# Expert results kept on chip: each turn of three blocks is multiplied by a table of tokens and added to the residual, in place of stores to memory and a gather at the end

## The reference, cut to what matters

```python
group_logits = xt @ rg_w + rg_b                       # 4 groups of 8 experts
grp = argmax(group_logits)
top_val, top_idx = lax.top_k(expert_logits[grp], 2)   # 2 experts of that group for each token
gate = p_grp * jax.nn.softmax(top_val)
...
out = zeros; for each (token, expert) chosen:
    out[token] += gate * ((silu(x @ w_gate[e]) * (x @ w_up[e])) @ w_down[e])
x = x + out
return rmsnorm(x, final_norm_g)
```

## Time and profile before

| | |
|---|---|
| median of 3 runs | 2055.2 us (2052.13 to 2055.3) |
| the profiled execution's own time | 2054.98 us |
| its span, first to last instruction | 2053.7 us |
| PE (TensorE) busy | 1824.7 us, 89% |
| DVE (VectorE) busy | 863.6 us, 42% |
| POOL (GpSimd) busy | 992.7 us, 48% |
| ACT (ScalarE) busy | 432.7 us, 21% |
| DMA | 346.00 MB, mean 168 GB/s |

### The profile page before, as it was taken

One profiled execution on the slowest core, in us unless ns is written; L12 is line 12 of the kernel. 1 busy time (PEld: TensorE's weight loads), 2 busy tenths in 40 slices (PEclk: granted clock), 3 DMA queues, 4 the chain that ended last, 5 costly groups with the idle time before them and its releaser, 6 DMA issues.

```text
span 2053.7 us, 27415 instructions
## 1 busy us (share of the span) xinstructions
PE 1824.7 (89%) x9686; PEld 1287.1 (63%) x9686; DVE 863.6 (42%) x1256; ACT 432.7 (21%) x794; POOL 992.7 (48%) x536
## 2 busy tenths in 40 slices
PE   5999999989999899999999798996877978969783
PEld 4888888877776578888888666664642423323331
DVE  5444443410254567444444489877341111111113
ACT  3111100100244432111100143551321211111112
POOL 5888887767544278888888523321211111101101
PEclk9999999999999999999999999997868988988897
DMA  3333363423221123333333222210579999999983
GB/s 126 97 97 93 105 262 98 141 79 98 66 62 52 32 85 95 97 93 101 92 109 98 72 60 64 72 52 21 212 287 412 374 408 402 410 415 398 413 358 133
DMA packets 56977, 346.00 MB, mean 168 GB/s; under 512 B 8474, under 2 KB 8858, under 8 KB 44896
## 3 DMA queue, kind: packets, MB, share of 16 engines
q1 hardware_dynamic: 44640, 315.12, 42.1%
q10 hardware_dynamic: 7968, 19.46, 2.6%
q0 software_dynamic: 4320, 10.78, 1.5%
HBM read 475.06 MB, written 19.66 MB: 241 GB/s over the span
## 4 chain that ended last, share of the span: by engine, by line
PE 70%; DMA 13%; DVE 11%; ACT 3%; issue 1%; POOL 1%; SPq 0%; DVEq 0%; ACTq 0%; POOLq 0%
PE bank L460 31%; DMA big<-w_up_in 13%; PE bank L431 12%; PE bank L1760 7%; PE bank L692 4%; PE bank L1266 3%; DVE big L1043 3%; PE bank L1778 2%; PE bank L479 2%; PE bank L1376 2%; PE bank L1786 1%; PE bank L610 1%; DVE state L1028 1%; PE bank L670 1%; PE bank L1678 1%
## 5 line engine op out<-in xcount | busy, mean ns | idle before, releaser
L277 POOL TENSOR_TENSOR weights_hi_parts<-ring,ones 128x1024 fp32r<-128x1024 f32 (+1 forms) x176 | 356.6, 2026 | 304.7 <-PE bank L460 139.1
L279 POOL TENSOR_TENSOR ring_parts<-ring,weights_hi_parts 128x1024 fp32r<-128x1024 f32 (+1 forms) x176 | 473.9, 2693 | 13.8
L460 PE MATMUL bank<-attention_buffers_parts,weights_hi_parts 128*128 128x512 f32 x832 | 329.4, 396 | 27.9 <-POOL ring_parts L279 17.6
L460 PE MATMUL bank<-state_parts,weights_hi_parts 128*128 128x512 f32 x832 | 326.8, 393 | 0.0
L460 PE MATMUL bank<-attention_buffers_parts,ring_parts 128*128 128x512 f32 x832 | 326.7, 393 | 0.0
L1760 PE MATMUL bank<-big,work 128*32 128x512 f32 x1440 | 231.7, 685 | 54.5 <-DMA big<-w_up_in 54.4
L431 PE MATMUL bank<-big_parts,weights_hi_parts 128*128 128x512 f32 x704 | 217.1, 389 | 1.2 <-POOL ring_parts L279 1.2
L460 PEld LDWEIGHTS bank<-attention_buffers_parts,weights_hi_parts 128*128 128x128 f32 x832 | 158.1, 190 | 64.6 <-POOL ring_parts L279 17.6
L864 POOL TENSOR_TENSOR ring_parts<-ring,weights_hi_parts 128x1024 fp32r<-128x1024 f32 x32 | 81.0, 2534 | 234.1 <-ACT weights_hi_parts L861 234.1
L1860 POOL TENSOR_TENSOR small<-small 128x1 f32<-128x1 f32 x51 | 9.7, 190 | 381.3 <-DVE small L1683 381.3
L460 PEld LDWEIGHTS bank<-state_parts,weights_hi_parts 128*128 128x128 f32 x832 | 158.3, 190 | 33.4 <-issue 0.8
(11 more groups left out here) (377 smaller groups left out, 2827.1 us busy)
## 6 DMA issues: line engine op xcount, KB each, us to landing
big<-w_up_in SPq DMA_DIRECT2D x54, 2048.0 KB
ring<-wdense_in SPq DMA_DIRECT2D x176, 512.0 KB, 3.6
state<-w_down_in SPq DMA_DIRECT2D x37, 2048.0 KB
big<-w_gate_in SPq DMA_DIRECT2D x36, 2048.0 KB
attention_buffers<-w_gate_in SPq DMA_DIRECT2D x18, 2048.0 KB
ring<-w_down_in SPq DMA_DIRECT2D x18, 2048.0 KB
ring<-wff_in SPq DMA_DIRECT2D x32, 704.0 KB, 4.1
y_rows<-big ACTq DMA_DIRECT2D x1, 8192.0 KB, 28.0
```

The lines of the kernel that those rows point to most:

```text
L277: po.tensor_tensor(hi, raw, ones[:, 0:1].to_broadcast([128, words]), ALU.mult).then_inc(PO.sem, 1)
L279: po.tensor_tensor(lo, raw, hi.bitcast(F32), ALU.subtract) \
L460: m = pe.matmul(out, x, y_, start=j + n == 0, stop=j == len(pairs) - 1 and n == len(ts) - 1)
```

## The change

Nothing of the results goes to memory any more. `y_rows`, its filling, the 108 stores and the eight gathers are gone. In their place:

- **Tables.** After the routing, VectorE works out for each chosen (token, expert) pair its turn and its row of 96 in that turn. Two tables of hits are multiplied on TensorE once, which gives for each turn and row the token's number and its gate.
- **A one-hot for each turn** (`dve_hot`): 96 rows by 512 tokens, 1 where the row belongs to the token, in fp32r, by VectorE.
- **Results of a turn stay in SBUF** (`lap_y`, 96 rows by 1024). `add_odd` writes them with two VectorE instructions for a block (one before).
- **Split** (`split_lap`): GpSimd multiplies the turn's results by their gates, once into a high fp32r part and once in place, and subtracts, for each half of 512 features: six instructions a turn. They begin when the turn's third block has its sum, and `dve_result` of the next turn's first block waits for both halves (`s_split`), since it overwrites `lap_y`.
- **Products** (`lap_sums`): TensorE multiplies the one-hot by the high and the low part, for four groups of 128 tokens and two halves: 16 fp32r matmuls a turn into three PSUM banks in rotation. They are placed around the next turn's second and third block: n = 0, 1 before and n = 2, 3 behind `turn_products` of the second block, n = 4, 5 behind `gate_up` of the third, n = 6, 7 behind its `down`.
- **Adds** (`dve_add`): VectorE adds each of the eight products to the residual, eight instructions a turn. Products n = 2 and 3 wait for the adds of n = 0 and 1, whose banks they reuse.
- **Order of the loops.** The first turn's blocks stand ahead of the loops, the loops run once less, and the last turn's body is written out behind them. GpSimd's gathers go on between the splits.
- **The end.** The last turn's results are multiplied as plain fp32: VectorE puts the gates into the one-hot (`last_hot`), TensorE makes eight matmuls into eight banks, VectorE adds each with one instruction of 512 columns, and the final norm goes on as before.

```diff
+    lap_high = nc.alloc_sbuf_tensor_at("lap_results_high", [128, D], F32R, offset=lap_high_at)
...
-    zeros = big[:, 44 * T:44 * T + D]
-    cleared = PO.run(po.memset(zeros, 0.0))
...
-        if gain == "mix_norm":
-            AC.wait(cleared)
-            ac.dma_start(y_d.rearrange("(n p) c -> p n c", p=128),
-                         zeros.unsqueeze(1).to_broadcast([128, Y_ROWS // 128, D])).then_inc(s_fill, 16)
...
+    DV.run(dv.tensor_scalar(lap.bitcast(I32), place, 43691.0, None, ALU.mult))
+    DV.run(dv.tensor_scalar(lap.bitcast(I32), lap.bitcast(I32), 17, None, ALU.logical_shift_right))
+    DV.run(dv.tensor_copy(lap, lap.bitcast(I32)))
+    DV.run(dv.scalar_tensor_tensor(lap_row, lap, float(-SETS), place, ALU.mult, ALU.add))
+    DV.run(dv.scalar_tensor_tensor(lap_row, lap_row, float(BS), rmod, ALU.mult, ALU.add))
...
+        if c >= 2:
+            pe.wait_ge(s_added, i * 8 + {2: 7, 3: 8, 4: 11, 5: 15}[c])
...
-    def act_odd(i, c):
+    def act_odd(i, c, steps=1):
 
         ac.wait_ge(PE.sem, at_step(PE, PE_D, i, c + 1))
+        if c:
+            ac.wait_ge(DV.sem, at_step(DV, DV_Y, i, c))
         ac.activation(y_odd, results[c % SETS][2 * BS:4 * BS, :], ACT.Copy).then_inc(AC.sem, 1)
 
-    def act_store(i, c):
-
-        ac.wait_ge(DV.sem, at_step(DV, DV_Y, i, c + 1))
-        store(i, c)
-
-    def store(i, c):
+    def add_odd(c):
 
         for half in range(2):
-            ac.dma_start(y_d[bass.ds(i * (SETS * BS) + c * BS, BS), half * 512:half * 512 + 512],
-                         y_e[c % SETS][half * BS:(half + 1) * BS, :]).then_inc(s_y[c % SETS], 16)
+            p = slice(half * BS, (half + 1) * BS)
+            d = dv.tensor_tensor(lap_y[c % SETS * BS:(c % SETS + 1) * BS, half * 512:half * 512 + 512],
+                                 results[c % SETS][p, :], y_odd[p, :], ALU.add)
+        return d
 
     def dve_result(i, c, steps=1):
 
         dv.wait_ge(AC.sem, at_step(AC, AC_Y, i, c + 1))
-        dv.wait_ge(s_y[c % SETS], i * 32 + (32 * (c // SETS) + 16))
-        dv.tensor_tensor(y_e[c % SETS], results[c % SETS][0:2 * BS, :], y_odd, ALU.add).then_inc(DV.sem, steps)
+        if c == 3:
+            dv.wait_ge(s_split, i * 2 + 2)
+        add_odd(c).then_inc(DV.sem, steps)
+
+    def dve_hot(i, lap_at):
+
+        dv.tensor_copy(sel[0:LAP, :], tab[0:LAP, lap_at]).then_inc(s_sel, 1)
+        dv.wait_ge(s_sel, i)
+        dv.tensor_tensor(lap_hot_r.rearrange("p (t n) -> p t n", t=NT), iota_f[0:LAP, :].unsqueeze(1).to_broadcast([LAP, NT, 128]),
+                         sel[0:LAP, 0:NT].unsqueeze(2).to_broadcast([LAP, NT, 128]), ALU.is_equal).then_inc(s_hot, 1)
+
+    def split_lap(i):
+
+        po.wait_ge(DV.sem, at_step(DV, DV_Y, i, 3))
+        gate = sel[0:LAP, NT:NT + 1].to_broadcast([LAP, 512])
+        for half in range(2):
+            y, high, low = (x[0:LAP, half * 512:half * 512 + 512] for x in (lap_y, lap_high, lap_low))
+            po.tensor_tensor(high, y, gate, ALU.mult).then_inc(s_high, 1)
+            po.tensor_tensor(y, y, gate, ALU.mult).then_inc(s_high, 1)
+            po.wait_ge(s_high, i * 4 + (2 * half + 2))
+            po.tensor_tensor(low, y, high.bitcast(F32), ALU.subtract).then_inc(s_split, 1)
+
+    sum_banks = [results[b] for b in (1, 2, 1, 2, 2, 0, 2, 0)]
+
+    def lap_sums(i, first):
+
+        for n in (first, first + 1):
+            if n == 0:
+                pe.wait_ge(s_hot, i + 1)
+            if n % 4 == 0:
+                pe.wait_ge(s_split, i * 2 + (n // 4 + 1))
+            if n == 5:
+                pe.wait_ge(DV.sem, at_step(DV, DV_Y, i, 4))
+            if n in (2, 3, 4, 6, 7):
+                pe.wait_ge(s_added, i * 8 + {2: 9, 3: 10, 4: 12, 6: 13, 7: 14}[n])
+            t, half = n % 4, n // 4
+            for part in (lap_high, lap_low):
+                m = pe.matmul(sum_banks[n][:, :], lap_hot_r[:, t * 128:(t + 1) * 128],
+                              part[0:LAP, half * 512:half * 512 + 512], start=part is lap_high, stop=part is lap_low)
+            m.then_inc(s_prod, 1)
+
+    def dve_add(i, first):
+
+        for n in (first, first + 1):
+            dv.wait_ge(s_prod, i * 8 + (n + 1))
+            d = x_half(n % 4, n // 4)
+            dv.tensor_tensor(d, d, sum_banks[n][:, :], ALU.add).then_inc(s_added, 1)
...
+    for c in range(SETS):
+        rows_to_come(0, c)
     with po.Fori(0, laps["po"]) as i:
-        for c in range(SETS):
-            po.wait_ge(PO.sem, i * SETS + (gathers_begun + c))
-            po.wait_ge(DV.sem, at_step(DV, DV_IDX, i, c - 1))
-            po.tensor_tensor(zo, zc, zc, ALU.add).then_inc(PO.sem, 1)
-            gather(c, idx[c][0:BS, :])
+        rows_to_come(i, 3)
+        rows_to_come(i, 4)
+        split_lap(i)
+        rows_to_come(i, 5)
+    split_lap(laps["po"])
+    po.wait_ge(PO.sem, laps["po"] * SETS + (gathers_begun + SETS))
...
+    lap_hits, row_hits = ring[:, 0:C2 * LAPS], ring[:, 512:512 + C2 * LAP]
+    row_values = ring[:, 168:168 + 2 * C2 * LAPS]
+    assert C2 * LAPS <= 168 and 168 + 2 * C2 * LAPS <= 512 and 512 + C2 * LAP <= RING * SLOT - WE
     dve_rows(0, 0)
+    dv.tensor_tensor(by_slot(lap_hits), iota_f[:, 0:LAPS].unsqueeze(1).to_broadcast([128, C2, LAPS]),
+                     over_last(lap, C2, LAPS), ALU.is_equal).then_inc(s_hits, 1)
+    dv.tensor_tensor(by_slot(row_hits), iota_f[:, 0:LAP].unsqueeze(1).to_broadcast([128, C2, LAP]),
+                     over_last(lap_row, C2, LAP), ALU.is_equal)
+    dv.wait_ge(s_hits, 1)
+    for k, v in enumerate((tok_id, gates)):
+        d = dv.tensor_tensor(row_values.rearrange("p (c n k) -> p c n k", c=C2, k=2)[:, :, :, k], by_slot(lap_hits),
+                             over_last(v, C2, LAPS), ALU.mult)
+    d.then_inc(s_hits, 1)
     dve_mul(0, 0, 2)
+    dve_rows(0, 1)
+    dve_result(0, 0)
+    dve_mul(0, 1)
+    dv.wait_ge(s_tab, 1)
+    tab3, summed = tab[0:LAP, :].rearrange("p (n k) -> p n k", k=NT + 1), results[2][0:LAP, 0:2 * LAPS].rearrange("p (n k) -> p n k", k=2)
+    for t in range(NT):
+        dv.tensor_scalar(tab3[:, :, t], summed[:, :, 0], float(NO_ROW - 128 * t), None, ALU.add)
+    dv.tensor_copy(tab3[:, :, NT], summed[:, :, 1]).then_inc(s_hits, 1)
+    dve_rows(0, 2)
+    dve_result(0, 1)
+    dve_mul(0, 2)
+    dv.wait_ge(s_hits, 3)
+    dve_hot(1, slice(0, NT + 1))
...
+    def dve_lap(i, last=False):
+
+        dve_rows(i, 3)
+        dve_result(i, 2)
+        dve_mul(i, 3)
+        dve_rows(i, 4)
+        dve_result(i, 3)
+        dve_add(i, 0)
+        dve_mul(i, 4)
+        dve_add(i, 2)
+        dve_add(i, 4)
+        if not last:
+            dve_rows(i, 5)
+        dve_result(i, 4, 3 if last else 1)
+        dve_add(i, 6)
+        dve_mul(i, 5)
+        dve_hot(i + 2, bass.ds(i * (NT + 1) + (NT + 1), NT + 1))
     with dv.Fori(0, laps["dv"]) as i:
-        for c in range(1, SETS + 1):
-            dve_rows(i, c)
-            dve_result(i, c - 1)
-            dve_mul(i, c)
-    dve_rows(laps["dv"], 1)
-    dve_result(laps["dv"], 0)
-    dve_mul(laps["dv"], 1)
-    dve_result(laps["dv"], 1, 3)
-    dve_mul(laps["dv"], 2)
-    dv.wait_ge(AC.sem, at_step(AC, AC_SILU, laps["dv"], 2) + 1)
-    dv.wait_ge(s_y[2], laps["dv"] * 32 + 16)
-    dv.tensor_tensor(y_e[2], results[2][0:2 * BS, :], y_odd, ALU.add).then_inc(DV.sem, 1)
+        dve_lap(i)
+    dve_lap(laps["dv"], last=True)
+    last_hot = work[0:LAP, 0:T]
+    dv.wait_ge(s_hot, laps["dv"] + 2)
+    dv.tensor_scalar(last_hot, lap_hot_r.bitcast(F32), sel[0:LAP, NT:NT + 1], None, ALU.mult)
+    dv.wait_ge(AC.sem, at_step(AC, AC_SILU, laps["dv"], 5) + 1)
+    add_odd(2).then_inc(DV.sem, 1)
...
+    pe.wait_ge(s_hits, 2)
+    product(results[2][0:LAP, 0:2 * LAPS],
+            [(row_hits[:, c * LAP:(c + 1) * LAP], row_values[:, c * 2 * LAPS:(c + 1) * 2 * LAPS]) for c in range(C2)]) \
+        .then_inc(s_tab, 1)
...
+    def pe_lap(i, last=False):
+
+        gate_up(i, 3)
+        next_rows(4)
+        down(i, 2)
+        turn_products(i, 3)
+        gate_up(i, 4)
+        next_rows(5)
+        down(i, 3)
+        lap_sums(i, 0)
+        turn_products(i, 4)
+        lap_sums(i, 2)
+        gate_up(i, 5, rows_next=not last)
+        lap_sums(i, 4)
+        if not last:
+            next_rows(6)
+        down(i, 4, 2 if last else 1)
+        lap_sums(i, 6)
+        turn_products(i, 5)
     with pe.Fori(0, laps["pe"]) as i:
-        for c in range(1, SETS + 1):
-            gate_up(i, c)
-            next_rows(c + 1)
-            down(i, c - 1)
-            turn_products(i, c)
-    gate_up(laps["pe"], 1)
-    next_rows(2)
-    down(laps["pe"], 0)
-    turn_products(laps["pe"], 1)
-    gate_up(laps["pe"], 2, rows_next=False)
-    down(laps["pe"], 1, 2)
-    turn_products(laps["pe"], 2)
-    down(laps["pe"], 2)
-
-
-    for b in range(SETS):
-        po.wait_ge(s_y[b], laps["po"] * 32 + 48)
-    po.wait_ge(PO.sem, laps["po"] * SETS + gathers_begun)
-    po.tensor_tensor(zo, zc, zc, ALU.add)
```

(20 more changed lines are left out.)

70 lines of the change are left out of this document (41 added, 29 removed).

## The result

| | before | changed kernel |
|---|---|---|
| median of the runs, us | 2054.65 (4 runs, 2052.13 to 2055.3) | 2100.41 (4 runs, 2089.8 to 2102.84) |
| profiled execution, us (span) | 2054.98 (2053.7) | 2089.80 (2088.5) |
| ratio | | 1.0215, interval 1.0184 to 1.0245 |

The changed kernel is 46 us slower, outside the range of the prediction (2036 to 2066).

What follows compares the result with a forecast made beforehand. The experts' stage was taken as bound by DMA until its last weight, then TensorE, then a serial end. 9.4 lost - 14.6 gained + 1.5 for small costs gave -3.7 on 2054.98; forecast 2051.5 us, 8 in 10 range 2036 to 2066.

Steps and rivals of the forecast that it cites:

- Part 1: The end after TensorE's last block: 18.8 us instead of 33.4, 14.6 us gained, bounds 12 to 16.
- Part 2: DMA's pace in the experts' stage: the removed stores free 17.6 us of all 16 engines, bounds 0 to 17.6.
- Part 3: TensorE's pace in the experts' stage: a turn of three blocks takes 21.2 + 6.3 = 27.5 us.
- Part 4: Experts' stage: bound moves from DMA to TensorE; sixteen turns 440 us, 5 more for unequal turns; 9.4 us lost.
- Part 5: Small parts: removed filling and ScalarE's dropped DMA issues give 0; tables hidden behind first weights, 3 us if not.
- C: Rival, chance 0.28: slower, as the chain over GpSimd to VectorE sets a longer turn; 2067 us at 28.5.
- B: Rival, chance 0.27: DMA keeps the pace, a turn on TensorE is 25.5 to 26.3 us; 2040 us.
- D: Rival, chance 0.05: the stores' DMA time is not given back, DMA's turn stays 27.3 us; 2057 us.

Runs made afterwards that it cites:

- e10: Kernel before without the two stores of each result, ScalarE raising the semaphore instead; run again for a profile: 2041.85 us, 0.9947 of before.
- e5: Kernel before without the two stores of each result, ScalarE raising the semaphore instead: 2039.4 us, 0.9925 of before.
- e1: Changed kernel plus nine unread fp32r matmuls a turn where TensorE otherwise waits for VectorE's first add: 2061.61 us, 1.0043 of before.
- e9: Changed kernel, split left on GpSimd, second to last sums moved behind third block's gate/up, down and transposed products: 2046.98 us, 0.9977 of before.
- e8: Changed kernel with the split on ScalarE (high part) and VectorE (low part) instead of GpSimd, TensorE's order unchanged: 2056.65 us, 1.0008 of before.
- e7: Changed kernel, split on ScalarE and VectorE, later sums spread behind third block's gate/up, down and transposed products: 2049.83 us, 0.9979 of before.
- e6: Kernel before plus 16 fp32r matmuls on zeros a turn, behind the third block's transposed products: 2063.56 us, 1.0047 of before.

## Why the prediction was wrong

**Part 1, the end: right in size, with two rows misread.** 19.2 us against 18.8 said, 33.4 before: 14.2 gained of 14.6. The first misreading is the pace of fp32 matmuls. One of them leaves two records (`lap_y` is multiplied by 8 calls and shows x16; so gate and up are 16 calls and down 8, not 32 and 16), and the two in 1.02 us are one matmul. The eight took 7.13 us, the first addition came 3.4 us behind the last down instead of 2.8, and what follows it 15.9 as said. The second is the clock. It fell 2.6 us behind the last matmul of the kernel before, not 12:
```profile
2020.30:2022.90 2.60, 0.03 (x4) 0.00 (x0) 0.68 (x1) 0.79 (x2) 0.00 (x0) 1.00 0.08 19
2022.90:2053.70 30.80, 0.00 (x0) 0.00 (x0) 16.42 (x20) 6.37 (x14) 8.17 (x9) 0.50 0.57 207
```
The mean of 0.54 over 33.4 us said so already. It cost nothing here (the clock was at 1.00 for the end's matmuls), but read rightly it would have warned part 3, whose working holds a stall of 2.7 us.

**Part 2, DMA's pace: the row was right, the use of it too hopeful.** 17.6 us was given as the value and 0 as the other bound; half to two thirds comes back (e10, e5). It had little weight in the result, since the changed kernel's turns hardly waited for DMA.

**Part 3, the turn: this step failed.** Its pieces stood up: matmuls at 0.23 us, the split in 6.72 us (6.9 said; subtractions 0.1 longer each and nearly no gaps, where six of 0.07 had been put in without a row), VectorE's sum 9.07 us behind the third block's down (9.2), gate and up of the next third block 13.2 us behind it (12.6). A turn of "21.2 + 6.3 = **27.5 us**" is what the trace shows, 27.6, but only in the turns where the clock stayed up, and in e1. The others are 30.7. The missing term is what the wait itself causes: TensorE had been put as busy or idle at one speed. Behind 2.12 us of idling the next matmuls and most of gate and up run at 1.2 GHz: 1.0 us more for four matmuls of sums and 2.3 for gate and up, 3.3 us, of which 3.1 are seen in the turn. The waits were in the working: the place was costed at 4.5 us, "of which 1.8 are matmuls", so 2.7 of stall, and nothing was said of what follows a stall. The row for it was on hand: gate and up behind a wait for DMA, 6.11 us, against 3.57. That wait was of 7.2 us, but the kernel before also has one as short as the new stall:
```profile
1924.39 5.07 PE L1760 MATMUL bank<-big,work 128*32 128x512 f32 x32 [2.02 <-DMA big<-w_up_in]
```
I used the clock for the end alone.

**Part 4, which pace wins: right in kind, short in size.** TensorE sets the pace and DMA's share fell to 0.86. But 440 + 5 us were said for the sixteen turns and 453.4 is what e1 takes at a clock of 0.99: the turns with many new experts cost 11.4 us over 27.6 (32.5, 30.5, 29.2 and 29.6), not 5, and 16 x 0.1 is the rest but for some rounding. Blocks ended at 2069.3, not 2029.7. The 39.6 us are: the clock 28.4, heavy turns and small differences of the turn 8.4, the last turn's tail 2.1 (14.2 instead of 12.1: gate and up 4.29 instead of 3.64, the last down 3.17 instead of 1.92), the start 0.7.

**Part 5: right.** The first block's gate and up start at 1521.6 us against 1522.0 before, and no wait for the tables is seen.

Of the **rivals**, C had the sign and its line ("from a turn of 27.8 on the kernel is slower"; 2067 at 28.5) but not the cause: GpSimd's split as a whole didn't run longer (6.72 us against 6.9). B (2040) had TensorE's turn near 26; e9 and its turn of 25.2 come to 2047. D was half true.

The Trainium skill has the missing term, in "TensorE: Matmul & The Clock Gate", HAM oscillation — how this bites in real kernels: a kernel whose TensorE waits once in every tile can have its clock taken down in every tile, so each begins slow. The trace agrees: gate and up take 5.0 to 6.0 us instead of 3.64 in 12 of the 16 third blocks of the first profile. The page tells it of longer waits, for DMA; here 2.12 us for an addition on VectorE were enough. The Trainium skill's rule that the prediction did weigh, "GPSIMD Engine Reference", Engine selection, would have kept the split off GpSimd. As a price it roughly holds: the page has GpSimd about twice as slow with two inputs, and here it took 1.03 to 1.27 us for 512 columns where VectorE took 0.68 to 0.74 (the low part in e8), 1.5 to 1.9 times. As advice it decides nothing here: e9 keeps the split there and stands to the kernel before as e7 does, which doesn't (0.9977 and 0.9979).

**Where the gain went.** In e9 the sixteen turns are 437.5 us, as before the change (437.2): what e10 gained there (9.1) and what e6 lost (10.5) nearly cancel. What is left is the end, from the start of the last turn's third block 34.1 us against 42.4 before, 8.3 of the 8.6 us between the two profiled executions. In the medians the change with its order right is worth less, 0.23% (0.13 to 0.33), 3 to 7 us.
